# Six pairs of column groups of the first feed-forward product computed with seven half-size products in place of eight

## What is computed

```python
def squared_relu_mlp(h, w1, w2):
    z = jax.nn.relu(h @ w1)
    return (z * z) @ w2

x = x + squared_relu_mlp(rms_norm(x, ffn_norm[i]), w_ff1[i], w_ff2[i])
```

## Time and profile before

| | |
|---|---|
| median of three runs | 2984.85 us |
| span of the profiled execution | 2982.6 us |
| TensorE products (PE) | 2945.8 us busy, 13140 |
| VectorE (DVE) | 1853.8 us busy |
| ScalarE (ACT) | 1493.9 us busy |
| GpSimd (POOL) | 635.6 us busy |
| moved by DMA | 611.34 MB, 205 GB/s over the span |

### The profile page before, as it was taken

One profiled execution on the slowest core, in us unless ns is written; L12 is line 12 of the kernel. 1 busy time (PEld: TensorE's weight loads), 2 busy tenths in 40 slices (PEclk: granted clock), 3 DMA queues, 4 the chain that ended last, 5 costly groups with the idle time before them and its releaser, 6 DMA issues.

```text
span 2982.6 us, 37047 instructions
## 1 busy us (share of the span) xinstructions
PE 2945.8 (99%) x13140; PEld 2425.4 (81%) x13140; DVE 1853.8 (62%) x2485; ACT 1493.9 (50%) x2004; POOL 635.6 (21%) x1257
## 2 busy tenths in 40 slices
PE   8999999999999999999999999999999999999998
PEld 7888888888888778788888888888888887878887
DVE  6537655546565777876555555556557777887555
ACT  6435444444344666655434444345444546775433
POOL 0003302213034210013303122133323673110210
PEclk9999999999999999999999999999999999999999
DMA  7546666666667655556666666676866786666774
GB/s 261 169 150 206 209 214 197 217 198 215 193 200 237 209 180 159 166 168 216 212 199 211 201 206 205 198 219 209 246 204 205 216 241 184 208 203 210 247 254 156
DMA packets 338542, 611.34 MB, mean 205 GB/s; under 512 B 37473, under 2 KB 62433, under 8 KB 337633
## 3 DMA queue, kind: packets, MB, share of 16 engines
q1 hardware_dynamic: 293392, 541.13, 58.1%
q0 software_dynamic: 44432, 67.45, 7.2%
q10 hardware_dynamic: 576, 0.94, 0.1%
HBM read 561.15 MB, written 10.49 MB: 192 GB/s over the span
## 4 chain that ended last, share of the span: by engine, by line
PE 87%; DVE 7%; ACT 3%; issue 1%; DMA 1%; DVEq 0%; ACTq 0%
PE acc L1935 28%; PE acc L1937 28%; PE acc L1936 28%; DVE wlo L1349 2%; DVE wlo L1344 1%; ACT whi L1016 1%; PE tp L2105 1%; DVE ob L1724 0%; PE sd L1999 0%; PE sd L2024 0%; DMA raw<-in_w_mem_kv 0%; PE tp L2095 0%; PE tp L1953 0%; ACT whi L1019 0%; PE tp L2055 0%
## 5 line engine op out<-in xcount | busy, mean ns | idle before, releaser
L1935 PE MATMUL acc<-whi,set_hi 128*128 128x512 f32 x4080 | 1607.5, 394 | 15.0 <-DVE wlo L1349 9.6
L1937 PE MATMUL acc<-whi,set_lo 128*128 128x512 f32 x4080 | 1589.3, 390 | 0.0
L1936 PE MATMUL acc<-wlo,set_hi 128*128 128x512 f32 x4080 | 1588.6, 389 | 0.0
L1349 DVE TENSOR_TENSOR wlo<-raw,whi 128x1024 fp32r<-128x1024 f32 x944 | 1133.4, 1220 | 711.9 <-ACT whi L1016 710.3
L1016 ACT ACTIVATE whi<-raw 128x1024 fp32r<-128x1024 f32 x944 | 981.7, 1058 | 926.4 <-PE acc L1937 659.3
L1935 PEld LDWEIGHTS acc<-whi,set_hi 128*128 128x128 f32 x4080 | 766.3, 188 | 190.9 <-DVE wlo L1349 18.2
L1937 PEld LDWEIGHTS acc<-whi,set_lo 128*128 128x128 f32 x4080 | 766.0, 188 | 161.6
L1936 PEld LDWEIGHTS acc<-wlo,set_hi 128*128 128x128 f32 x4080 | 766.5, 188 | 157.7 <-issue 1.9
L983 POOL DMA_DIRECT2D u<-u x832 | 407.6, 498 | 1470.0 <-DVE u L1472 1379.6
L1344 DVE SCALAR_TENSOR_TENSOR wlo<-raw,par,whi 128x512 fp32r<-128x512 f32 x160 | 111.6, 746 | 47.1 <-ACT whi L1019 46.4
L1019 ACT ACTIVATE whi<-raw,par 128x512 fp32r<-128x512 f32 x160 | 104.3, 715 | 22.6 <-PE acc L1937 11.2
(11 more groups left out here) (276 smaller groups left out, 1274.1 us busy)
## 6 DMA issues: line engine op xcount, KB each, us to landing
raw<-in_w_ff SPq DMA_DIRECT2D x512, 512.0 KB, 4.5
raw<-in_w_in SPq DMA_DIRECT2D x248, 512.0 KB, 4.5
raw<-in_w_out SPq DMA_DIRECT2D x96, 512.0 KB, 4.4
u<-u POOLq DMA_DIRECT2D x832, 32.0 KB, 4.6
raw<-in_w_mem_kv SPq DMA_DIRECT2D x32, 512.0 KB, 4.7
raw<-in_w_proj_a SPq DMA_DIRECT2D x32, 512.0 KB, 4.4
raw<-in_w_proj_b SPq DMA_DIRECT2D x32, 512.0 KB, 6.7
raw<-in_w_kv SPq DMA_DIRECT2D x48, 256.0 KB, 3.3
```

The lines of the kernel that those rows point to most:

```text
L1349: V.tensor_tensor(wlo[:, c], raw[:, c], whi[:, c].bitcast(f32), ALU.subtract).then_inc(w_lo, 1)
L1935: T.matmul(o, h[:, tok], whi[:, c], start=first, stop=False)
L1936: T.matmul(o, h[:, tok], wlo[:, c], start=False, stop=False)
L1937: ins = T.matmul(o, l[:, tok], whi[:, c], start=False, stop=last)
```

## The change

Take two neighbouring column groups of w_ff1. With the activations cut into two halves of the inner dimension and two token blocks, and the weights into two halves of rows and the two groups, their product is a 2 x 2 by 2 x 2 block product. It needs eight half-size block products; the scheme of Strassen in Winograd's form needs seven. In chunks 1 to 3 of both layers ("halved" chunks), groups 0 and 1 are made so; groups 2 and 3 stay. Six pairs in all.

- **Parts.** The seven stages p1, p2, p5, p3, p6, p7, p4 have four parts each. A part is a slab of 512 KB with one token block: 6 products. The 28 parts of a pair are each put behind one ordinary slab, from slab 8 of the w_ff2 groups of the chunk before; the last four (p4) stand behind slabs 0 to 3 of the halved chunk.
- **Activation sums** are made once a layer on VectorE and ScalarE, beside chunk 0 (`sum_full`, `sum`, `sum_hi`, `sum_lo`).
- **Weight sums.** p1 is loaded into four own buffers (`chain_raw`); POOL then issues transfers that add the next block of the weight to it, for p5, p6 and p4 (`chain_add`). p2, p3 and p7 are loaded into the ring; for p7 VectorE subtracts the ring's slab from the chain's (`u3`), two tasks ahead.
- **Combinations** of the seven results: `part_p1`, `part_p5`, `part_p7` on ScalarE, `part_c11`, `part_q`, `part_n2`, `part_n1` on VectorE; then relu, square and turn as before. `n2` is the second group's output and `n1` the first's; the table in `ffn` gives the slabs of their steps.
- **Hardware loops** go: all engines run plain code (class `N`, `loops`, `loop_slab`, `loads` are removed).

```diff
+    def number_all(self):
+
+        taken = [0] * RAW
+        for v in range(NSLAB * len(self.groups)):
+            for part in [None] + self.parts.get(v, []):
+                t = Task(len(self.stream), v // NSLAB, v % NSLAB, part)
+                if part is None:
+                    of, _, _, _ = self.slab_of(t.g, t.s)
+                    taken[t.slot] += SLAB_K if self.groups[of].pieces else 1
+                else:
+                    part.n = t.n
+                    taken[t.slot] += part.stage not in CHAIN
+                t.loads = taken[t.slot]
+                self.stream.append(t)
+        self.number = {NSLAB * t.g + t.s: t.n for t in self.stream if t.part is None}
...
+STAGES = ("p1", "p2", "p5", "p3", "p6", "p7", "p4")
+CHAIN = {"p1": 0, "p5": 1, "p6": 2, "p4": 3}
+BLOCKS = {"p1": (0, 0), "p2": (1, 0), "p5": (0, 1), "p3": (1, 1), "p6": (1, 1), "p7": (0, 0), "p4": (1, 0)}
+SUMS = {"p5": 0, "p7": 1, "p3": 2, "p6": 3}
+QUARTERS = NK // 2 // SLAB_K
+START = 8
...
-        first = sc.group(f"w_ff1{layer}", 0, 0, a)
-        sc.fed_late(first)
-        sc.loops[first + 1] = dict(layer=layer, tail0=sc.tails, staged0=sc.staged, turn0=sc.turns, rst=rst, a=a, z=z)
-        for _ in range(8 * (NCHUNK - 1)):
-            sc.group(None, 0, 0, a)
-        sc.tails += 4 * (NCHUNK - 1)
-        sc.turns += 4 * (NCHUNK - 1)
-        sc.staged += 4 * (NCHUNK - 1)
-        c = NCHUNK - 1
-        prev = len(sc.groups) - 1
-        gs = [prev] + [sc.group(f"w_ff1{layer}", 0, D * c + GW * i, a) for i in range(1, 4)]
-        for i, g in enumerate(gs):
-            sc.epilogue(g, "relu2", rst, sc.staged, sc.tails)
-            sc.turned(S * (g + 1) + 1, S * (g + 2) + 1, ("staged", sc.staged), z, 4 * i)
-            sc.staged += 1
-        fs = [sc.group(f"w_ff2{layer}", D * c, GW * i, z) for i in range(4)]
-        sc.weave(fs[0], fs[1], FF2_PAIR)
-        for n, left in ((0, 2), (4, 1), (12, 0)):
-            sc.groups[fs[n // S]].need[n % S] = [("tail_lo", sc.tails - left)]
-        for i, g in enumerate(fs):
-            e = sc.end(g)
-            sc.epilogue(g, "add", GW * i)
-            sc.at("act", e + 2, "x_stat", next_rst, i, g)
-            if i < 3:
-                sc.turned(e + 2, e + (12 if i == 1 else 9), ("x", i, g), a, 4 * i, next_gain, room=f"u{i % 2}")
+        for c in range(NCHUNK):
+            halved = c > 0
+            gs = [sc.group(f"w_ff1{layer}", 0, D * c + GW * i, a) for i in range(2 if halved else 0, 4)]
+            if c == 0:
+                sc.fed_late(gs[0])
+                for n in range(4):
+                    sc.at("dve", S * gs[0] + 9 + n, "sum_full", n, sc.tails)
+                for n in range(5):
+                    sc.at("dve", S * gs[0] + 14 + 2 * n, "sum", n)
+                for n in range(4):
+                    sc.at("act", S * gs[0] + (15, 17, 21, 23)[n], "sum_hi", layer, n)
+                    sc.at("dve", S * gs[0] + (17, 19, 23, 25)[n], "sum_lo", layer, n)
             else:
-                sc.tail(e + 3, e + 5, ("x", i, g), a, 4 * i, next_gain)
+                v = S * gs[0]
+                for of, kt, add, relu, square, split in (("n2", 0, 0, 1, 2, 6), ("n1", 4, 4, 5, 6, 11)):
+                    sc.at("dve", v + add, "part_" + of, p)
+                    sc.at("act", v + relu, "relu_" + of, p, rst)
+                    sc.at("dve", v + square, "part_square", p, of, sc.staged, sc.tails)
+                    sc.turned(v + square, v + split, ("staged", sc.staged), z, kt)
+                    sc.staged += 1
+                    if of == "n2":
+                        sc.at("act", v + 3, "part_p7", p, sc.staged)
+            for i, g in enumerate(gs):
+                turn = S * (g + 1) + (3 if halved and i == 0 else 1)
+                sc.at("act", S * (g + 1) + 1, "epi_relu2", g, rst, sc.staged, sc.tails)
+                sc.at("dve", turn, "epi_relu2", g, rst, sc.staged, sc.tails)
+                sc.turned(turn, S * (g + 2) + 1, ("staged", sc.staged), z, 4 * i + (8 if halved else 0))
+                sc.staged += 1
+            fs = [sc.group(f"w_ff2{layer}", D * c, GW * i, z) for i in range(4)]
+            sc.weave(fs[0], fs[1], FF2_PAIR)
+            if c < NCHUNK - 1:
+                v = S * fs[0] + START
+                p = sc.pair_of(layer, c + 1, a, v)
+                sc.at("act", v + 6, "part_p1", p)
+                sc.at("act", v + 14, "part_p5", p)
+                sc.at("dve", v + 9, "part_c11", p)
+                sc.at("dve", v + 21, "part_q", p)
+            for n, left in ((0, 2), (4, 1), (12, 0)):
+                sc.groups[fs[n // S]].need[n % S] = [("tail_lo", sc.tails - left)]
+            for i, g in enumerate(fs):
+                e = sc.end(g)
+                sc.epilogue(g, "add", GW * i)
+                if c < NCHUNK - 1:
+                    continue
...
+            def part_load(task):
+                part = task.part
+                if part.stage in CHAIN:
+                    if part.stage != "p1":
+                        return
+                    pair = sc.pairs[part.pair]
+                    if pair.first:
+                        sp.wait_ge(sm["sum_lo"], 4 * (pair.layer + 1))
+                    else:
+                        sp.wait_ge(w_lo, sc.pairs[part.pair - 1].parts["p4", part.j].n + 1)
+                    sp.dma_start(in_rows(chain_raw[part.j]), block_of(part, "p1"))\
+                        .then_inc(sm[f"chain_in{part.j}"], 16)
+                    return
+                sp.wait_ge(w_lo, task.n + 1 - RAW)
+                sp.dma_start(in_rows(raw[:, task.slot * SLAB:(task.slot + 1) * SLAB]), block_of(part, part.stage))\
+                    .then_inc(ld[task.slot], 16)
...
+            def chain_add(part):
+
+                after = {"p1": "p5", "p5": "p6", "p6": "p4"}[part.stage]
+                pool.wait_ge(w_lo, part.n + 1)
+                if after == "p4":
+                    pool.wait_ge(sm["u3_ok"], QUARTERS * part.pair + part.j + 1)
+                dma(in_rows(chain_raw[part.j]), block_of(part, after), accum_op=mybir.AluOpType.add)\
+                    .then_inc(sm[f"chain_add{part.j}"], 16)
...
+                elif task.part.stage in ("p1", "p5"):
+                    chain_add(task.part)
+                elif task.part.stage == "p7":
+                    chain_add(sc.pairs[task.part.pair].parts["p6", task.part.j])
...
+            def hi(task, fold=None):
+                part, n = task.part, task.n
+                c = slice(task.slot * SLAB, (task.slot + 1) * SLAB)
+                src = raw[:, c]
+                if part and part.stage in CHAIN:
+                    act.wait_ge(*chained(part, part.stage))
+                    src = chain_raw[part.j]
+                elif part and part.stage == "p7":
+                    act.wait_ge(sm["u3_ok"], QUARTERS * part.pair + part.j + 1)
+                else:
+                    act.wait_ge(ld[task.slot], 16 * task.loads)
+                if n >= RAW:
+                    act.wait_ge(mm, n + 1 - RAW)
...
+            def part_p7(p, staged):
+
+                act.wait_ge(mm, sc.pairs[p].last("p7"))
+                act.wait_ge(sm["staged"], staged)
+                A_(stage_a[:, GW:2 * GW], bank_b, ACT.Copy).then_inc(sm["part_p7"], 1)
+
+            def relu_n2(p, k):
+
+                act.wait_ge(sm["rstd_ok"], k + 1)
+                act.wait_ge(sm["part_n2"], p + 1)
+                for b in range(TB):
+                    t = stage_a[:, GW * b:GW * (b + 1)]
+                    ins = A_(t, t, ACT.Relu, scale=minus_rstd[:, b:b + 1])
+                ins.then_inc(sm["part_relu"], 1)
...
+            def u3(task):
+
+                c = slice(task.slot * SLAB, (task.slot + 1) * SLAB)
+                dve.wait_ge(ld[task.slot], 16 * task.loads)
+                dve.wait_ge(*chained(task.part, "p6"))
+                V.tensor_tensor(raw[:, c], chain_raw[task.part.j], raw[:, c], ALU.subtract).then_inc(sm["u3_ok"], 1)
...
+            def part_q(p):
+
+                dve.wait_ge(mm, sc.pairs[p].last("p6"))
+                dve.wait_ge(sm["part_p5"], p + 1)
+                V.tensor_tensor(mixed_c[:], bank_a, mixed_c[:], ALU.add).then_inc(sm["part_q"], 1)
+
+            def part_n2(p):
+
+                dve.wait_ge(mm, sc.pairs[p].last("p7"))
+                dve.wait_ge(sm["part_q"], p + 1)
+                V.tensor_tensor(stage_a[:, 0:GW], bank_d, mixed_c[:], ALU.add)
+                V.tensor_tensor(stage_a[:, GW:2 * GW], bank_b, mixed_c[:], ALU.add).then_inc(sm["part_n2"], 1)
+
+            def part_n1(p):
+
+                dve.wait_ge(mm, sc.pairs[p].last("p4"))
+                dve.wait_ge(sm["part_p7"], p + 1)
+                t = stage_a[:, GW:2 * GW]
+                V.tensor_tensor(t, bank_a, t, ALU.add).then_inc(sm["part_n1"], 1)
+
+            def part_square(p, of, q, tails):
+
+                dve.wait_ge(sm["part_relu"], 2 * p + (1 if of == "n2" else 2))
+                dve.wait_ge(sm["tail_tp"], tails)
```

(84 more changed lines are left out.)

376 lines of the change are left out of this document (172 added, 204 removed).

## The result

The changed kernel takes 3086.86 us in the median (3083.99 to 3094.64), against 2984.68 us (2984.25 to 2986.6) for the kernel before on the same chip: a ratio of 1.0346, 95% interval 1.0331 to 1.036. It is slower by 102 us. The forecast was slower by 44 us, 3029 us, with a range that ended at 3058: the direction is right, the size is wrong, and the time lies outside the range.

A forecast was written before the change was run, and what follows sets the result against it. The prediction took TensorE, busy 2945.8 of 2982.6 us, as the bound. Its terms, -32.6 + 60.9 + 10 + 6 = +44.3 us on the median of 2984.85, gave 3029 us, range 2970 to 3058.

The forecast's parts named there:

- The removed products: On TensorE, six pairs lose 144 products at 0.2267 us each: 32.6 us saved.
- Edits at nothing: Extra slab splits, u3 subtractions, combinations, activation sums and plain code for loops: taken as zero, sums at worst 1 us per layer.
- The turned tiles: In halved chunks, later slab splits queue behind turned tiles' landings: 10.15 us of waits per chunk, 4.7 lost net of savings.
- late starts: POOL sometimes starts a shuffle 3.1 us late; some 2 of 18 shuffles: 6 us, ends 0 and 12.
- The p7 stage and the adding transfers: In p7, u3 waits for its own load and delays splits: 1.7 us per pair, 10 us in all.
- the price of a transfer: Accumulating 512 KB, shown by no row: 1.33 us as a plain transfer, 2.65 us if the destination is also read.
- L = 6.5: Landing time in us assumed for slab loads in p7; beside heavy traffic they took 5.2 to 7.6 us.
- the prediction's own period: VectorE's time for two tasks in p7, (3 x 1.22 + L)/2 with landing time L; 4.08 us at L = 4.5.
- the lead: Slabs are split ahead of TensorE's use: 5.8 us with whole slabs, 3.0 us or more where parts alternate with slabs.
- The second rival: Accumulating transfers cost double, 2.65 us: 3048 us, with p1's too 3060 and more; above 3040, with slower parts, chance 0.17.
- The faster rival: The turned tiles' trip is short, 10.9 us with landings of 1.7 us: 2952 to 2979 us, chance 0.20.
- The Trainium skill's fit for one transfer: About 2.0 us plus bytes over 436 GB/s: 32 KB land in 2.1 us, trip 11.3 us, kernel near 2971 us.

The follow-up runs named there:

- e5: Changed kernel without accumulating transfers (weight sums left out), with later turned-tile steps and the first two second-product groups woven in thirds: 2954.48 us, ratio 0.9901.
- e9: Changed kernel, everything computed, accumulating transfers kept, with later turned-tile steps and the first two second-product groups woven in thirds: 3041.3 us, ratio 1.0193.
- e2: Changed kernel without its 72 accumulating transfers and the waits for them, so the weight sums are left out: 3015.68 us, ratio 1.0109.
- e6: Changed program with no pair: four ordinary groups in every chunk, plain code for hardware loops, old turned-tile schedule: 2984.63 us, ratio 1.0.
- e3: Changed kernel with the 72 accumulating transfers as plain writes of the same bytes, the sums not formed: 3019.04 us, ratio 1.0112.

## Why the prediction was wrong

The two causes, by the spans of the profiled executions, each taken away in either order:

| | span, us | step |
|---|---|---|
| before | 2982.6 | |
| e5: neither cause | 2952.4 | -30.2 |
| e9: adding transfers alone | 3038.1 | +85.7 |
| changed: both | 3092.8 | +54.7 |
| e2: the steps alone, over e5 | 3010.1 | +57.7 |

**The removed products, -32.6:** right. e5 has 30.2 of them.

**Edits at nothing** (splits, combinations, activation sums, loops): right. e5 leaves 2.4 us for all of them; e6 shows the loops alone at zero.

**The turned tiles, +60.9 and +6 for late starts:** right in mechanism and near in size, 54.7 to 57.7 for 66.9. With 63.8 us for 54.4 it loses 9.4 us in this chunk, late issue included, where 10.15 without late issues were forecast; six times that is 56 us. In this chunk the products at half clock between its links add nothing to this: behind the slow products TensorE comes to wait for VectorE again (560 to 565 above), so the chain, not the products, decides when it goes on.

**The p7 stage and the adding transfers, +10:** this is the step that failed. It measured 83 to 86 us. Three things in it were wrong.

First, the price of a transfer. The prediction said that no row shows it, gave 1.33 and 2.65 us as ends, and took the lower. It is 2.96 us, over the upper end. The demand in p7 is then 2 x 1.65 + 2.96 = 6.3 us of all engines in each 4.08 us. Also 1.33 us was low for the plain transfers: it divided by the highest rate seen, while the queue's share gives 1.65.

Second, the landing time. It was one number, L = 6.5, and the sum's steps are sensitive to it. In the stage itself, 470 to 484 us, the changed kernel and then e5:

```profile
raw<-in_w_ff SPq DMA_DIRECT2D x5, 512.0 KB, 9.5
```

```profile
raw<-in_w_ff SPq DMA_DIRECT2D x5, 512.0 KB, 4.3
```

By the prediction's own period, (3 x 1.22 + 9.5) / 2 = 6.6 us for each two tasks in place of 4.08: 10 us behind in four, less the 3 us of lead, 7 us. This pair did lose 7 us there, but not quite in that way: TensorE waited 4.0 us (0.24 and 3.76 in the windows at 480 and 485), and most of the other 3 us were products at half clock behind the wait. From VectorE's first split of a chain buffer in one stage to that of the next (L1448, L1443 in e5), changed kernel, then e5:

```profile
383.23 1.23 DVE L1448 TENSOR_TENSOR wlo<-qk,whi 128x1024 fp32r<-128x1024 f32 x1 [1.21 <-ACT whi L1090]
...
420.44 1.22 DVE L1448 TENSOR_TENSOR wlo<-qk,whi 128x1024 fp32r<-128x1024 f32 x1
...
457.39 1.23 DVE L1448 TENSOR_TENSOR wlo<-qk,whi 128x1024 fp32r<-128x1024 f32 x1
...
501.19 1.21 DVE L1448 TENSOR_TENSOR wlo<-qk,whi 128x1024 fp32r<-128x1024 f32 x1
```

```profile
383.15 1.23 DVE L1443 TENSOR_TENSOR wlo<-qk,whi 128x1024 fp32r<-128x1024 f32 x1 [1.49 <-ACT whi L1085]
...
417.15 1.23 DVE L1443 TENSOR_TENSOR wlo<-qk,whi 128x1024 fp32r<-128x1024 f32 x1
...
449.79 1.23 DVE L1443 TENSOR_TENSOR wlo<-qk,whi 128x1024 fp32r<-128x1024 f32 x1
...
486.56 1.22 DVE L1443 TENSOR_TENSOR wlo<-qk,whi 128x1024 fp32r<-128x1024 f32 x1
```

p6 with p7 takes 43.8 us for 36.8: 7.0 more. But p1 to p5 takes 37.2 for 34.0, and p5 to p6 36.95 for 32.6. That is the third error: the lead was said to cover the p1 burst, and the p5 burst, whose backlog falls into p3, was not counted at all. Together 3.2 + 4.3 + 7.0 = 14.5 us in this pair. The pairs differ: from the first p1 product to the first p4 product they take 108.9 to 113.4 us each, 97.9 in e5, and the six together lose 83.2 us, 20.6 in p1 and p2, 28.3 in p5 and p3, 34.3 in p6 and p7. That is the measured 83 to 86. The second rival named this cause but costed it at 3048 us, or 3060 with p1: it held p3 at nothing too, and stopped at 2.65 us.

Some of these 83 to 86 us are the clock. e9 has no chain and is still busy for 2944.9 us, 31.7 above 2913.2, and e5, with no long waits, for 2914.1. The prediction's sum took every wait as its length; here 85.7 us divide into 30.8 us of longer busy time (by the mean clock, 0.991 for 0.999, at most 24 of them half clock) and 54.9 of idle time (93.2 in e9, 38.3 in e5). In p7 slow products do lengthen the stage: at its end VectorE has caught up and waits 3.31 us for TensorE's last product (the row at 499.98).

**The faster rival** (a short trip, 2952 to 2979 us) fell with the first profile: from turn to set_hi it was 12.4 to 15.4 us in the three links above (508.11 to 523.52 the longest, 527.01 to 539.43 the shortest), as the earlier trace rows had said. The Trainium skill's fit for one transfer, page "DMA: Bandwidth & Descriptors", section "Anatomy of one DMA — SWDGE (gpsimd) path", would by the prediction's estimate have left 1.4 us of waits in the chunk. The chain lost 9.4: the fit does not hold for the last transfer of a shuffle.

What stays open: whether the addition costs the engines their time by a read of the destination, by smaller packets or otherwise. e3 and the changed kernel differ in this alone, and the packets of q0 do rise with it (54800 to 64016, 128 more for each of the 72) at the same megabytes, but nothing here tells the two apart. Nor is there a run that changed the spacing of the bursts.
